# Eight unused columns between two buffers of the second model

## The chip, the cores and the metric

The kernel runs on one core of one Trainium2 chip. The metric is the device time of one launch in microseconds (us), the median of several runs. Engines are named as the profile names them: PE is the matrix engine (PEld its weight loads), DVE the vector engine, ACT the scalar engine, POOL the GpSimd engine, SP the queue that issues most transfers.

## The reference

Two models run one after the other, all in float32, on 256 tokens of width 1024, two layers each.

The first block projects x with `w_in` and runs four branches (a recurrent one, a latent attention, a convolution, a cross-attention into a memory), gates and adds them, projects with `w_out` and normalises. The second block takes its result, and a context of 256 more tokens beside it. Cut to what matters here:

```python
def swiglu(h, w1, w2):
    gate, up = jnp.split(h @ w1, 2, axis=-1)
    return (jax.nn.silu(gate) * up) @ w2

def ffn_sublayer(h, m, sub, g_pre, g_post, w1, w2):
    shift, scale, gate = mods_of(m, sub)
    y = swiglu(modulate(rms_norm(h, g_pre[sub]), shift, scale), w1, w2)
    return h + MACARON_WEIGHT * gate * rms_norm(y, g_post[sub])

def hybrid_layer(x, xc, ...):
    x, xc = ffn_sublayer(x, ..., 0, ...), ffn_sublayer(xc, ..., 0, ...)
    ...                      # projections h @ w_in, three kinds of attention, o @ w_out
    x = ffn_sublayer(x, ..., 2, ...)
    ...                      # the same for xc, in the first layer alone
```

The inner width of the feed-forward part is 22 x 128 = 2816.

## The kernel before, in words

**Products in parts.** The type `fp32r` is a rounded float32 that PE takes at a faster rate. To keep the precision, every large product of the second model is made of three: a weight panel is split into a high part and a low part (the rest), the activations likewise, and high x high, high x low and low x high are added in one bank of PSUM. In `parts` these are lines L1830, L1831 and L1832: the weights are the stationary operand, which is loaded anew for every matmul, and the activations the moving one, of 512 columns (the tokens of x and of the context) or of 256.

```python
1828            def parts(out, w, w_low, a, a_low, start, stop):
...
1830                mm(out, w, a, start=start, stop=False)
1831                mm(out, w, a_low, start=False, stop=False)
1832                return mm(out, w_low, a, start=False, stop=stop)
```

`mm(out, stationary, moving)`. In the second half of a feed-forward part, and in the output projection of an attention, the roles are changed: `rows_tile` (matmul on L1913) has the activations (`hs`, or `aT` and `aT_low`) stationary and 512 columns of the split weights `ws` moving. The first model does the same with its own buffers on L477 (`xT` moving), L478 (`xT_low` moving) and L479 (`xT` moving), with `ws` stationary and 256 columns each. Its other matmuls, such as L444 and L454, are plain float32.

**Flow of a panel.** A panel is 128 x 2048 float32 (1 MB). SP brings it into one of two slots of `ring`; POOL waits for it and for the matmuls that used the slot of `ws` last (`come`, L1758 is a one-element operation after the wait), writes the high part (L1745) and then the low part (L1747) and raises `split_in`; PE waits for `split_in` and does 48 matmuls. From the second panel of the last feed-forward part on (`SHARED`), POOL makes only half of the low part (L1763, L1765), and DVE the other half (L2445). PE counts `used` up at a panel's last matmul, and this lets POOL split the panel after the next.

**Order of the stages in the second model.** For each layer: feed-forward with 22 panels of `unit_panel` (the first two in `lead`, which starts on 256 tokens while the other 256 are still being normalised) and 11 panels of `rows_tile`; the attention, with 8 panels of projections (again behind a `lead`), 2 of values, plain float32 matmuls on `hidT`, `prob` and `y`, and 4 panels of `rows_tile`; and a feed-forward part again. The last one has 256 tokens instead of 512.

**Where the buffers lie.** Buffers are laid out one behind the other in every partition, in the order of their declarations. The second model's are:

```python
1635        ring = sb("ring", [P, 2, PAN])
1636        ws = sb("ws", [P, 2, 2, PAN], F32R)
1637        y = sb("y", [P, 4, D])
1638        aT = sb("aT", [P, KD, T2], F32R)
1639        hidT = sb("hidT", [P, FF, T2])
```

and then `sg`, `rows`, `bias`, `aT_low`, `prob` (in one place with `hs`), `gsc`, `gg`, `gg_rows` and `small`. Byte addresses in a partition, in the built programs, and the rest on division by 64:

| buffer | role in split products | address | mod 64 |
|---|---|---|---|
| second model `ws` | weights' parts | 54048 | 32 |
| `y` | (not in split products) | 86816 | 32 |
| `aT` | activations, high | 103200 | 32 |
| `aT_low` | activations, low | 189216 | 32 |
| `hs` | hidden activations, both parts | 205600 | 32 |
| first model `ws` | weights' parts | 153216 | 0 |
| first model `xT` | activations, high | 107296 | 32 |
| first model `xT_low` | activations, low | 202368 | 0 |

Inside a buffer, every operand of these matmuls starts a whole multiple of 512 bytes behind the buffer's start, so all operands of a buffer share its rest. The plain float32 matmul of L454 has `brT` (116640) and `ring` (25376), both with rest 32.

Of the kernel before, what the change touches and what calls it, by code (L numbers as in the profile page):

```python
# [15 lines left out]
P = 128  # L16
# [1610 lines left out]
def second_model(nc, io, x_tok, mod, early, out):  # L1627

    with ExitStack() as ctx:
        def sb(name, shape, dt=F32):  # L1630
            return ctx.enter_context(nc.sbuf_tensor("m2_" + name, shape, dt))
# [3 lines left out]
        ring = sb("ring", [P, 2, PAN])  # L1635
        ws = sb("ws", [P, 2, 2, PAN], F32R)
        y = sb("y", [P, 4, D])
        aT = sb("aT", [P, KD, T2], F32R)
        hidT = sb("hidT", [P, FF, T2])
        sg = sb("sg", [P, 2, T2])  # L1640
# [982 lines left out]
def program(nc, io, out):  # L2623

    with ExitStack() as ctx:
        x_tok = ctx.enter_context(nc.sbuf_tensor("x_tok", [P, NT, D], F32))
        mod = ctx.enter_context(nc.sbuf_tensor("mod", [P, DEPTH * 9 * KD * 2], F32))
        early = {"vec": ctx.enter_context(nc.sbuf_tensor("m2_vec", [P, NVEC2], F32)),
                 "con": ctx.enter_context(nc.sbuf_tensor("m1_con", [P, NCON], F32)),
                 "mem": ctx.enter_context(nc.sbuf_tensor("memT_ctx", [P, NT * D], F32)),  # L2630
                 "loaded": ctx.enter_context(nc.semaphore("m2_loaded"))}
        first_model(nc, io, x_tok, mod, early)
        second_model(nc, io, x_tok, mod, early, out)
# [16 lines left out]
```

How the kernel before makes its waits and increments, by code:

```python
        @block.sync  # L336
# [12 lines left out]
            sp.dma_start(early["vec"][:, :], io["vec2"]).then_inc(early["loaded"], 16)  # L349
            def panels(g0, g1):
                with sp.Fori(g0, g1) as g:
                    for p in range(RING):
                        sp.wait_ge(s["panel_used"], (g - 1) * RING + p + 1)
                        sp.dma_start(ring[:, p, :], io["panels1"][bass.ds(g * RING + p, 1), :, :]
                                     .rearrange("o p n -> p (o n)")).then_inc(slot[p], 16)
            panels(1, PANELS1 // RING)
            for n in range(PANELS1, PANELS1 + RING):
                sp.wait_ge(s["panel_used"], n - RING + 1)
                if n == PANELS1:
                    sp.dma_start(ring[:, 0, 0:PAN // 2], io["panels1"][n, :, 0:PAN // 2]).then_inc(s["first_in"], 16)
                    sp.dma_start(ring[:, 0, PAN // 2:], io["panels1"][n, :, PAN // 2:]).then_inc(slot[0], 16)
                else:
                    sp.dma_start(ring[:, n % RING, :], io["panels1"][n, :, :]).then_inc(slot[n % RING], 16)
            panels(PANELS1 // RING + 1, DEPTH * PANELS1 // RING)
            sp.dma_start(early["mem"][:, :].rearrange("p (i d) -> p i d", d=D), io["ctx"]).then_inc(early["loaded"], 16)
            if out is not None:
                sp.wait_ge(s["layer_done"], DEPTH + 1)
                sp.dma_start(out[0, :, :].rearrange("(i p) d -> p i d", p=P), x_tok[:, :, :]).then_inc(s["out_st"], 16)
                sp.wait_ge(s["out_st"], 16)
```

## Time and profile before

| | |
|---|---|
| time, median of 3 runs | 2860.42 us (2859.85 to 2860.79) |
| span of the profiled execution | 2857.6 us |
| PE busy, share of the span | 96% |
| PE weight loads busy | 80% |
| POOL / DVE / ACT busy | 47% / 36% / 23% |
| DMA | 390.24 MB, mean 137 GB/s |

The profiled execution has its span alone, not a device time of its own beside it; the median of the three runs is 2.8 us longer than the span. The recorded duration of a matmul includes its way through the array, so matmuls overlap and their rate is read from their starts, not from their durations.

### The profile page before, as it was taken

To read this page: it belongs to the slowest core of one execution; us is meant where nothing else is said; L and a number is where in the kernel's file an instruction comes from. 1 tells how busy PE (TensorE), PEld (TensorE's weight loads), DVE (VectorE), ACT (ScalarE), POOL (GpSimd) and SP (SyncE) were. 2 spreads that over 40 slices of the span, in tenths; PEclk is the share of its full clock that TensorE was granted. 3 is DMA by queue.
4 is the path that set the end of the run, shared out by engine and by line. 5 is a ranking of instruction groups with operands and counts; after the bars stand their busy time and mean duration, and the time that the engine had idled before them with its cause. 6 is when DMAs were issued, how large, how long until landed. Compare 5 with 4: busy or idle time off the path is not lost.

```text
span 2857.6 us, 44212 instructions
## 1 busy us (share of the span) xinstructions
PE 2737.9 (96%) x17521; PEld 2281.5 (80%) x17521; DVE 1019.0 (36%) x1586; ACT 656.3 (23%) x1220; POOL 1342.8 (47%) x608
## 2 busy tenths in 40 slices
PE   8999999999999897999999999999999999898998
PEld 7987778699777775888888778888888888776996
DVE  1752753247438333001340533002330023524237
ACT  4432212144322112000131443001130001415101
POOL 4830100067010003565646555666646666667786
PEclk9999999999999998999999999999999999999999
DMA  6556633445565444323222123222223222232453
GB/s 231 187 193 249 258 141 134 183 177 187 224 238 209 160 163 120 110 94 103 88 89 103 45 67 104 90 101 94 98 89 103 90 101 97 96 117 71 151 171 138
DMA packets 68621, 390.24 MB, mean 137 GB/s; under 512 B 19232, under 2 KB 20864, under 8 KB 22528
## 3 DMA queue, kind: packets, MB, share of 16 engines
q1 hardware_dynamic: 66640, 379.03, 37.1%
q10 hardware_dynamic: 1840, 9.18, 0.9%
q8 instruction: 106, 1.74, 0.2%
q14 instruction: 35, 0.29, 0.0%
HBM read 387.09 MB, written 1.10 MB: 136 GB/s over the span
## 4 chain that ended last, share of the span: by engine, by line
issue 26%; POOL 11%; POOLq 10%; PE 9%; DMA 3%; DVE 1%; SPq 1%; ACT 0%; DVEq 0%; ACTq 0%
POOL m_ws L1747 9%; POOLq L1746 7%; DMA m_ring<-in_panels 3%; PE m_bank L1913 2%; POOLq L1759 1%; PE m_bank L1830 1%; POOL m_ws L1765 1%; PE m_bank L1831 1%; PE m_bank L1832 1%; POOLq L1764 1%; PE m_bank L2046 1%; SPq L1703 1%; PE m_bank L2058 1%; PE m_bank L2009 1%; PE m_bank L2010 1%
## 5 line engine op out<-in xcount | busy, mean ns | idle before, releaser
L1830 PE MATMUL m_bank<-m_aT,m_ws 128*128 128x512 f32 (+1 forms) x1792 | 631.4, 352 | 34.8 <-DVE m_aT_low L2408 15.6
L1831 PE MATMUL m_bank<-m_aT_low,m_ws 128*128 128x512 f32 (+1 forms) x1792 | 628.0, 350 | 0.0
L1832 PE MATMUL m_bank<-m_aT,m_ws 128*128 128x512 f32 (+1 forms) x1792 | 627.7, 350 | 0.0
L1747 POOL TENSOR_TENSOR m_ws<-m_ring,m_ws 128x2048 fp32r<-128x2048 f32 x127 | 593.5, 4673 | 18.7
L1913 PE MATMUL m_bank<-m_ws,m_hs 128*128 128x512 f32 x1848 | 422.6, 390 | 3.5 <-DVE m_ws L2445 1.5
L1830 PEld LDWEIGHTS m_bank<-m_aT,m_ws 128*128 128x128 f32 x1792 | 344.9, 192 | 82.2 <-issue 23.6
L1913 PEld LDWEIGHTS m_bank<-m_ws,m_hs 128*128 128x128 f32 x1848 | 346.1, 188 | 79.4 <-issue 6.9
L383 POOL TENSOR_TENSOR m_ws<-m_ring,m_ws 128x2048 fp32r<-128x2048 f32 x48 | 221.3, 4627 | 342.4 <-ACT m_ws L910 342.4
L1831 PEld LDWEIGHTS m_bank<-m_aT_low,m_ws 128*128 128x128 f32 x1792 | 345.1, 193 | 42.4
L1832 PEld LDWEIGHTS m_bank<-m_aT,m_ws 128*128 128x128 f32 x1792 | 344.9, 192 | 42.6
L2451 DVE TENSOR_TENSOR m_hidT<-m_sg,m_bank 128x512 f32 (+3 forms) x88 | 54.7, 621 | 687.6 <-ACT m_sg L2218 687.6
L1758 POOL TENSOR_TENSOR m_small<-m_small 128x1 f32<-128x1 f32 x158 | 31.9, 202 | 546.5 <-PE m_bank L1832 366.4
L1745 POOL TENSOR_SCALAR m_ws<-m_ring 128x2048 fp32r<-128x2048 f32 x127 | 243.4, 1916 | 24.9 <-issue 20.0
L444 PE MATMUL m_bank<-m_xF,m_ring 128*128 128x256 f32 x1024 | 229.1, 382 | 4.2 <-DMA m_ring<-in_panels 4.2
L444 PEld LDWEIGHTS m_bank<-m_xF,m_ring 128*128 128x128 f32 x1024 | 191.9, 190 | 46.6 <-issue 12.1
L2218 ACT ACTIVATE m_sg<-m_bank 128x512 f32<-128x512 f32 (+1 forms) x88 | 48.0, 545 | 764.4 <-PE m_bank L1832 764.4
L2458 DVE TENSOR_TENSOR m_hs<-m_hidT,m_hs 128x512 fp32r<-128x512 f32 (+1 forms) x88 | 144.9, 1657 | 206.5 <-ACT m_hs L2222 206.1
L477 PE MATMUL m_bank<-m_xT,m_ws 128*128 128x256 f32 x752 | 212.2, 282 | 1.4 <-ACT m_work L928 1.4
L479 PE MATMUL m_bank<-m_xT,m_ws 128*128 128x256 f32 x752 | 212.8, 283 | 0.0
L478 PE MATMUL m_bank<-m_xT_low,m_ws 128*128 128x256 f32 x752 | 209.0, 278 | 0.0
L477 PEld LDWEIGHTS m_bank<-m_xT,m_ws 128*128 128x128 f32 x752 | 141.4, 188 | 3.2 <-ACT m_work L928 3.0
L478 PEld LDWEIGHTS m_bank<-m_xT_low,m_ws 128*128 128x128 f32 x752 | 141.3, 188 | 0.2
(350 smaller groups left out, 3412.9 us busy)
## 6 DMA issues: line engine op xcount, KB each, us to landing
m_ring<-in_panels SPq DMA_DIRECT2D x350, 1024.0 KB, 4.9
m_rows<-m_gg_dram ACTq DMA_DIRECT2D x6, 1024.0 KB, 5.4
m_bias<-in_rpb SPq DMA_DIRECT2D x48, 64.0 KB, 2.7
m_ring<-in_panels SPq DMA_DIRECT2D x4, 512.0 KB, 5.4
m_hT<-in_ln_rows ACTq DMA_DIRECT2D x2, 1024.0 KB, 6.8
m_con<-in_con SPq DMA_DIRECT2D x1, 1536.0 KB, 10.7
memT_ctx<-in_memT SPq DMA_DIRECT2D x2, 512.0 KB, 5.6
x_tok<-in_x SPq DMA_DIRECT2D x1, 1024.0 KB, 13.6
```

Source lines behind the costliest of these rows:

```text
L383: nc.gpsimd.tensor_tensor(ws[:, c_ % 3, 1, :], ring[:, PANEL[("in", c_)] % RING, :], ws[:, c_ % 3, 0, :].bitcast(F32), ALU.subtract).then_ ...
L444: last = mm(out[:, u * T:(u + 1) * T], w[:, u, k, :], xF[:, k, :], start=(k == 0), stop=(k == KD - 1))
L477: mm(dst, w[:, 0, u, k, :], xT[:, k, :], start=(k == 0), stop=False)
L478: mm(dst, w[:, 0, u, k, :], xT_low[:, k, :], start=False, stop=False)
L479: last = mm(dst, w[:, 1, u, k, :], xT[:, k, :], start=False, stop=(k == KD - 1))
L1745: nc.gpsimd.tensor_scalar(ws[:, p, 0, :], ring[:, p, :], 1.0, 0.0, ALU.mult, ALU.add)
L1746: pool.drain()
L1747: nc.gpsimd.tensor_tensor(ws[:, p, 1, :], ring[:, p, :], ws[:, p, 0, :].bitcast(F32), ALU.subtract)\
L1830: mm(out, w, a, start=start, stop=False)
L1831: mm(out, w, a_low, start=False, stop=False)
L1832: return mm(out, w_low, a, start=False, stop=stop)
L1913: last = mm(bank[:, 2 * i + hf, :], lhs[:, at], rhs[:, hf * 512:(hf + 1) * 512], start=start and q == 0, stop=stop and q == 2)
```

## The change

One declaration is added, of eight float32 columns (32 bytes in a partition) that nothing reads or writes:

```diff
@@ -1635,6 +1635,7 @@
         ring = sb("ring", [P, 2, PAN])
         ws = sb("ws", [P, 2, 2, PAN], F32R)
         y = sb("y", [P, 4, D])
+        sb("between", [P, 8])
         aT = sb("aT", [P, KD, T2], F32R)
         hidT = sb("hidT", [P, FF, T2])
         sg = sb("sg", [P, 2, T2])
```

`aT`, `hidT`, `sg`, `rows`, `bias`, `aT_low`, `prob`, `hs` and all behind them move by 32 bytes: `aT` to 103232, `aT_low` to 189248 and `hs` to 205632, each with rest 0 on division by 64. `ring`, `ws` and `y` of the second model, and all buffers of the first, stay. No instruction is added, removed or moved on any engine; lines behind L1637 have a number that is higher by one.

## Rows read from the trace of the kernel before

**Rows 1.** Page: span, and busy time of the engines.

```profile
span 2857.6 us, 44212 instructions
PE 2737.9 (96%) x17521; PEld 2281.5 (80%) x17521; DVE 1019.0 (36%) x1586; ACT 656.3 (23%) x1220; POOL 1342.8 (47%) x608
```

**Rows 2.** Groups on PE by shape: line, out<-in, shape xcount | busy us, mean ns | idle before.

```profile
L1830 PE MATMUL m_bank<-m_aT,m_ws 128*128 128x512 f32 x1088 | 423.8, 390 | 6.7 <-POOL m_ws L1747 3.8 <-DVE m_hidT L2451 2.9
...
L1913 PE MATMUL m_bank<-m_ws,m_hs 128*128 128x512 f32 x1848 | 422.6, 390 | 3.5 <-DVE m_ws L2445 1.5 <-issue 1.3 <-POOL m_ws L1765 0.5
...
L1830 PE MATMUL m_bank<-m_aT,m_ws 128*128 128x256 f32 x704 | 207.6, 295 | 28.2 <-DVE m_aT_low L2408 15.6 <-POOL m_ws L1747 6.0 <-POOL m_ws L1765 4.6
...
L1913 PE MATMUL m_bank<-m_ws,m_aT 128*128 128x512 f32 x192 | 53.0, 398 | 1.8 <-POOL m_ws L1747 1.8
```

**Rows 3.** Timeline of PE, 1200:1240: start us, duration; 174 matmuls lie between these starts.

```profile
1199.90 0.39 PE L1830 MATMUL m_bank<-m_aT,m_ws 128*128 128x512 f32 x1
...
1239.34 0.39 PE L1830 MATMUL m_bank<-m_aT,m_ws 128*128 128x512 f32 x1
```

**Rows 4.** Timeline of PE, 1499:1511, 256 columns; 87 matmuls from start to start.

```profile
1498.87 0.28 PE L1830 MATMUL m_bank<-m_aT,m_ws 128*128 128x256 f32 x1
...
1509.31 0.28 PE L1830 MATMUL m_bank<-m_aT,m_ws 128*128 128x256 f32 x1
```

**Rows 5.** Timeline of PE, 1362:1400, 169 matmuls merged into one row.

```profile
1361.74 38.47 PE L1913 MATMUL m_bank<-m_ws,m_hs 128*128 128x512 f32 x169
```

**Rows 6.** Timeline of PE, 507:520, plain float32, 62 matmuls in one row.

```profile
506.80 13.54 PE L454 MATMUL m_bank<-m_brT,m_ring 128*128 128x256 f32 x62
```

**Rows 7.** Timeline of PE, 60:75, first model; 126 matmuls from start to start.

```profile
60.06 0.28 PE L477 MATMUL m_bank<-m_xT,m_ws 128*128 128x256 f32 x1
...
74.90 0.28 PE L477 MATMUL m_bank<-m_xT,m_ws 128*128 128x256 f32 x1
```

**Rows 8.** Timeline of PE, 105:107, first model, four matmuls in a row.

```profile
105.09 0.28 PE L478 MATMUL m_bank<-m_xT_low,m_ws 128*128 128x256 f32 x1
105.20 0.28 PE L479 MATMUL m_bank<-m_xT,m_ws 128*128 128x256 f32 x1
105.32 0.28 PE L477 MATMUL m_bank<-m_xT,m_ws 128*128 128x256 f32 x1
105.44 0.28 PE L478 MATMUL m_bank<-m_xT_low,m_ws 128*128 128x256 f32 x1
```

**Rows 9.** Timeline of PE, 1724:1725, with the clock granted at half speed.

```profile
1723.98 0.41 PE L1830 MATMUL m_bank<-m_aT,m_ws 128*128 128x256 f32 x1
1724.20 0.41 PE L1831 MATMUL m_bank<-m_aT_low,m_ws 128*128 128x256 f32 x1
```

**Rows 10.** Timeline of POOL, 1800:1825, a feed-forward part with 512 tokens; [idle before <- what ended it].

```profile
1805.49 0.19 POOL L1758 TENSOR_TENSOR m_small<-m_small 128x1 f32<-128x1 f32 x1 [3.86 <-PE m_bank L1832]
1805.84 1.92 POOL L1745 TENSOR_SCALAR m_ws<-m_ring 128x2048 fp32r<-128x2048 f32 x1 [0.16 <-issue]
1807.91 4.60 POOL L1747 TENSOR_TENSOR m_ws<-m_ring,m_ws 128x2048 fp32r<-128x2048 f32 x1
```

**Rows 11.** Timeline of all engines, 1748.9:1751.2, end of a lead.

```profile
1748.99 0.28 PE L1832 MATMUL m_bank<-m_aT,m_ws 128*128 128x256 f32 x1
...
1750.72 0.49 PE L1830 MATMUL m_bank<-m_aT,m_ws 128*128 128x512 f32 x1 [1.45 <-DVE m_hidT L2451]
```

**Rows 12.** Timeline of PE, last feed-forward part: starts of three panels.

```profile
2697.39 0.38 PE L1830 MATMUL m_bank<-m_aT,m_ws 128*128 128x256 f32 x1 [0.32 <-POOL m_ws L1765]
...
2703.24 0.28 PE L1830 MATMUL m_bank<-m_aT,m_ws 128*128 128x256 f32 x1
...
2709.48 0.38 PE L1830 MATMUL m_bank<-m_aT,m_ws 128*128 128x256 f32 x1 [0.32 <-POOL m_ws L1765]
```

**Rows 13.** Timeline of POOL in the same stretch.

```profile
2703.49 0.19 POOL L1758 TENSOR_TENSOR m_small<-m_small 128x1 f32<-128x1 f32 x1 [0.55 <-PE m_bank L1832]
...
2709.25 0.19 POOL L1758 TENSOR_TENSOR m_small<-m_small 128x1 f32<-128x1 f32 x1
```

## The prediction

> **What bounds the kernel now.** I read the page first: PE is busy for 96% of the span, no other engine for more than half [rows 1]. So what counts is how long PE takes for one matmul, and where something else sets the pace. The groups by shape show where PE's time lies in the second model: 1088 matmuls of 512 columns on each of L1830, L1831 and L1832 with `aT` or `aT_low` moving, 704 of 256 columns on each, and 1848 + 192 on L1913 with `ws` moving [rows 2]. Idle time stands before few of them: 6.7 us before the 512-column ones.
>
> Then the timeline of PE, for the rate. With 512 columns, 174 matmuls take 1239.34 - 1199.90 = 39.44 us, 226.7 ns each [rows 3]; with 256 columns, 87 take 10.44 us, 120.0 each [rows 4]. L1913 runs at (38.47 - 0.39) / 168 = 226.7 as well [rows 5]. At 2.4 GHz 512 columns last 213.3 ns and 256 columns 106.7. Both forms therefore pay 13.3 ns over their columns, 32 columns' worth. Plain float32 shows that this isn't the price of loading weights: 62 matmuls with as many weight loads take 13.54 us; with about 0.4 taken off for the last one's own length (0.39 in [rows 3]), 61 steps of 215 ns each [rows 6], only 2 over the 213.3 of two passes over 256 columns. Nor is it paid at the lower clock: 0.22 us from start to start where 256 columns at 1.2 GHz last 213.3 ns [rows 9]. What is paid looks like the fetching of fp32r operands, which at the full clock takes as long as the array, or longer.
>
> **What 32 bytes are worth.** The buffers of the second model all have rest 32 on division by 64; the change makes the activations' 0. The trace of before has one place with other rests: the first model, with `ws` at 0, `xT` at 32 and `xT_low` at 0. There 126 matmuls of the same 256 columns take 14.84 us, 353.3 ns for each three [rows 7], not 360.0. So a rest does matter: a group of three with one moving operand at 0 is 6.7 ns shorter, just 16 columns, which are 64 bytes. My reading is that the moving operand is fetched in pieces of 64 bytes: one that starts at rest 32 touches one piece more (17 instead of 16, or 33 instead of 32), and each piece lasts 16 columns, 6.67 ns. Every matmul then pays one piece, and one with the moving operand at rest 32 two. All three counts come out: 3 x (106.7 + 13.3) = 360, 2 x 120.0 + 113.3 = 353.3, and 213.3 + 13.3 = 226.7. Where the starts can be told apart it is L478, the one with `xT_low`, that is short: 0.11 us to the next start, the others 0.12 [rows 8]. The first model's float32 matmuls, with both operands at 32, pay nothing because each column there lasts two passes, which hides the piece.
>
> The Trainium skill weighs against this. Its page "TensorE: Matmul & The Clock Gate", section "Wait — 56ns, not 53.3ns?", gives N / 2.4 + about 2.5 ns for a warm matmul, wherever its operands lie; [rows 3] has 226.7 where that would give 215.8, so it doesn't describe these fp32r matmuls. Its page "SBUF — State Buffer", section "Specifications (TRN2)", has lines of 16 bytes; a shift of 32 bytes would then change nothing. That would make the time of before, and is counted as a rival.
>
> **The sum.** L1913 keeps its moving operand `ws` at 32, and gets nothing; the same holds for all of the first model and all plain float32. For L1830 to L1832:
>
> 1. 512 columns: 3 x 1088 = 3264 matmuls x 6.67 = **21.8 us**. All of it should be seen: a panel is 48 x 226.7 = 10.88 us, POOL splits one in 0.19 + 0.16 + 1.92 + 0.15 + 4.60 = 7.0 and then waits 3.86 us for PE [rows 10]. A panel of 10.56 us leaves it 3.5. ACT and DVE wait for PE there too, since 6.7 us in all is PE's idle time before these [rows 2].
> 2. Five leads with 4 x 48 = 192 matmuls of 256 columns, at most 960 x 6.67 = 6.4 us. But the last 48 of a lead are followed by a wait, 1748.99 to 1750.72 [rows 11], because POOL could begin only at the end of the 48 before them; it needs its 7.0 us against 48 x 120 = 5.76, so what those 48 gain the wait takes. The first ones run at the lower clock [rows 9] or wait for DVE (15.6 us in all [rows 2]). I count half of the rest, 72: 72 x 6.67 = 0.48 us, five times: **2.4 us**, with bounds of 0 and 6.4.
> 3. 96 matmuls of 256 columns in the second attention: two panels of 5.76 us, under POOL's 7.0, so **0**.
> 4. The last feed-forward part, 22 panels of 48 matmuls with 256 columns. Here PE and POOL alternate: two panels last 2709.48 - 2697.39 = 12.09 us [rows 12]. POOL starts at 2703.49, when PE's panel ends, and has done at 2709.25, 5.76 us later; PE goes on after it at 2709.48 [rows 12, 13]. The ring is one panel of PE (5.76), one of POOL (5.76), and 0.57 for handing over. A panel that is 0.32 shorter makes it 11.77; two panels of POOL, 11.52, still fit. So half of the 0.64 is got: 10.5 pairs x 0.32 = **3.4 us**, with bounds of 0 and 7.0.
>
> Together 21.8 + 2.4 + 3.4 = 27.6 us off the profiled execution's span of 2857.6, which gives 2830.0, and with the 2.8 us around it **2832.8**. By the bounds this case alone lies between 2860.4 - 35.2 = 2825.2 and 2860.4 - 21.8 = 2838.6.
>
> What else moves is DVE's, ACT's and POOL's operands in `hidT`, `sg`, `prob` and `hs`, and the targets of the `bias` and `rows` transfers. No row compares two rests for these. I count nothing: beside the 512-column matmuls they lie under PE's work, which idles 6.7 us there. Where that cover is gone PE idles before L1830 for 28.2 us in the whole kernel, 15.6 of them for DVE [rows 2]; a tenth more or less of it would be 3 us either way.
>
> **The rivals.**
>
> *It is the distance between stationary and moving operand that matters* (they meet in the same place of the memory when the rests are equal). Then the first model's three are 2 q + 120.0 = 353.3, so q = 116.7, 3.3 less. After the change both kinds of matmul have unequal rests: 3264 x 3.33 = 10.9, L1913 2040 x 3.33 = 6.8, leads 1.2, the last part 1.7; 20.6 in all, **2839.8**. Against it: L478, with equal rests, would be the long one of the three, and it is the short one [rows 8]. The skill's TensorE page, section "Step-by-step: what each phase is for", has separate ports for the two operands, which would also exclude it; no run here shows ports. Chance 0.17.
>
> *Nothing changes.* The first model's 353.3 may come from something other than rests (its three slots of `ws`, its PSUM halves), or the piece is 128 bytes or more long, and rest 64 is as bad as rest 32; against the last speaks that 128 bytes would cost 32 columns. Here also: only the stationary operand's rest counts, 120.0 - 117.8 = 2.2 ns each, and only L1913's moves, 2040 x 2.2 = 4.5 us, 2855.9. **2860**, 2856 to 2861, chance 0.22.
>
> *Slower: a matmul pays more when its two operands have different rests.* Suppose that L478 in the first model, with both at 0, costs the bare 106.7 + 2; then L477 and L479 cost (353.3 - 108.7) / 2 = 122.3, 2.3 more than 120.0. After the change all split matmuls of the second model are of that kind: 3264 x 2.3 + 2040 x 2.3 = 12.2, leads 1, last part 1 (POOL's ring as above): 14 us, **2874.5**. It makes the kernel slower by over 0.2% from 0.9 ns a matmul on. For it: 0.12 against 0.11 [rows 8] fits it as well. Chance 0.08.
>
> *The forecast*: 0.50. The rest of 0.03 is for gains that meet an unseen wait.
>
> **How the numbers follow.** The forecast and the first rival are both faster: 0.67, with 0.02 of the rest 0.69. No change (2856 to 2861) holds 0.22, and slower, with 0.01 of the rest, 0.09. 0.2% is 5.7 us, about what a measurement of this kernel tells from no change. The range has to take in the forecast's bounds (from 2825), the first rival and no change to leave out less than 2 in 10: 2824 to 2861. The likeliest case's own range is 2825 to 2839.
>
> **What the profile would show.** Step by step: L1831 (now L1832) to the next start 220.0 ns with 512 columns, 660 for three, where 680 stood; 113.3 with 256; L1913 (now L1914) still 226.7. If L1914 falls to about 223 and the others to 223 too, it was the distance. POOL's wait [rows 10] shrinks from 3.86 to 3.5 us; the wait behind a lead grows from 1.7 to 2.0; the pair of panels [rows 12] becomes 11.8. The forecast is wrong if the 512-column matmuls stay at 226.7, or if they fall while POOL or DVE gets slower by as much.

## The result and the profile after

The changed kernel takes 2891.04 us (median of 4 runs, 2888.13 to 2891.84), the kernel before 2860.14 in the same comparison: a ratio of 1.0108, with a 95% interval of 1.0094 to 1.0123. It is slower by 31 us; 2832.8 was forecast, and a range up to 2861.

The page has the same instructions, 32.4 us more span and 28 us more of PE; DVE, ACT and POOL are as busy as before to 2.3 us [rows 1]:

```profile
span 2890.0 us, 44212 instructions
PE 2766.1 (96%) x17521; PEld 2273.6 (79%) x17521; DVE 1016.9 (35%) x1586; ACT 656.8 (23%) x1220; POOL 1345.1 (47%) x608
```

In the groups on PE by shape (all lines behind L1637 are one higher) both kinds of 512-column matmul have grown, `aT` moving from 390 to 395 ns and `hs` stationary from 390 to 396, while the idle time before them has grown by 0.8 us in all [rows 2]:

```profile
L1914 PE MATMUL m_bank<-m_ws,m_hs 128*128 128x512 f32 x1848 | 433.9, 396 | 3.8 <-DVE m_ws L2446 1.8 <-issue 1.5 <-POOL m_ws L1766 0.5
L1831 PE MATMUL m_bank<-m_aT,m_ws 128*128 128x512 f32 x1088 | 430.3, 395 | 7.2 <-POOL m_ws L1748 7.2
```

The timeline of PE gives the rate. First `aT` moving, 512 columns: 171 matmuls from start to start take 39.90 us, 233.3 ns each, where it was 226.7 [rows 3]. Then 256 columns, 63 matmuls in 7.42 us, 117.8 each, where it was 120.0 [rows 4]. Then one merged row of L1914: (42.40 - 0.39) / 180 = 233.4, where it was 226.7 [rows 5]:

```profile
1200.06 0.40 PE L1831 MATMUL m_bank<-m_aT,m_ws 128*128 128x512 f32 x1
...
1239.96 0.39 PE L1831 MATMUL m_bank<-m_aT,m_ws 128*128 128x512 f32 x1
...
1512.00 0.28 PE L1831 MATMUL m_bank<-m_aT,m_ws 128*128 128x256 f32 x1
...
1519.42 0.28 PE L1831 MATMUL m_bank<-m_aT,m_ws 128*128 128x256 f32 x1
...
1367.82 42.40 PE L1914 MATMUL m_bank<-m_ws,m_hs 128*128 128x512 f32 x181
```

So a matmul of 512 columns lost 6.7 ns and one of 256 gained 2.2. The loss stands in 3264 + 2136 matmuls (1848 with `hs`, 192 with `aT` and 96 with `aT_low` stationary) and in 192 more, L2009 to L2011 of before, which have `aT` and `aT_low` stationary too; those went from 227.2 to 233.2 ns. Of the 5592, the 264 of the last feed-forward part took 65.3 us before and 66.1 now, 0.8 more. The others make 5328 x 6.67 = 35.5 us, 36.3 together. The gain is small: two panels of the last feed-forward part start 12.02 us apart instead of 12.09 [rows 12], in all 0.7 us, and the five leads can give back 960 x 2.2 = 2.1 at most. These sums leave 33.5 us for a span that grew by 32.4. POOL's wait per panel went from 3.86 us up to 4.16, while its own longest operation stayed at 4.60 to 4.63 [rows 10]: the growth is PE's.

```profile
2729.63 0.38 PE L1831 MATMUL m_bank<-m_aT,m_ws 128*128 128x256 f32 x1 [0.46 <-POOL m_ws L1766]
...
2741.65 0.38 PE L1831 MATMUL m_bank<-m_aT,m_ws 128*128 128x256 f32 x1 [0.45 <-POOL m_ws L1766]
```

The first model's buffers have not moved. Yet in this execution 126 of its matmuls take 14.98 us, 356.7 ns for three, where the kernel before had 353.3 in the same stretch [rows 7]:

```profile
59.97 0.28 PE L477 MATMUL m_bank<-m_xT,m_ws 128*128 128x256 f32 x1
...
74.95 0.28 PE L477 MATMUL m_bank<-m_xT,m_ws 128*128 128x256 f32 x1
```

That is half of the 6.7 ns from which the forecast was drawn, with nothing changed there. From 94 us on, in the same execution, the same lines take 353.3 again.

### The profile page after: what moved, and what is told of

The parts are those of the page before. It is cut to its first block, busy times and chain, and to the rows that moved or that the text cites. A ratio compares the mean times of both kernels' runs of the same rounds, so it can differ in the third digit from the quotient of the medians.

```text
span 2890.0 us, 44212 instructions
## 1 busy us (share of the span) xinstructions
PE 2766.1 (96%) x17521; PEld 2273.6 (79%) x17521; DVE 1016.9 (35%) x1586; ACT 656.8 (23%) x1220; POOL 1345.1 (47%) x608
## 4 chain that ended last, share of the span: by engine, by line
issue 27%; POOL 11%; POOLq 10%; PE 9%; DMA 3%; DVE 1%; SPq 1%; ACT 0%; DVEq 0%; ACTq 0%
POOL m_ws L1748 9%; POOLq L1747 7%; DMA m_ring<-in_panels 3%; PE m_bank L1914 2%; POOLq L1760 1%; PE m_bank L1831 1%; PE m_bank L1833 1%; PE m_bank L1832 1%; POOL m_ws L1766 1%; POOLq L1765 1%; PE m_bank L2047 1%; SPq L1704 1%; PE m_bank L2059 1%; PE m_bank L2010 1%; PE m_bank L2012 1%
## 5 line engine op out<-in xcount | busy, mean ns | idle before, releaser
L1831 PE MATMUL m_bank<-m_aT,m_ws 128*128 128x512 f32 (+1 forms) x1792 | 635.4, 355 | 36.6 <-DVE m_aT_low L2409 15.6
L1914 PE MATMUL m_bank<-m_ws,m_hs 128*128 128x512 f32 x1848 | 433.9, 396 | 3.8 <-DVE m_ws L2446 1.8
L1914 PEld LDWEIGHTS m_bank<-m_ws,m_hs 128*128 128x128 f32 x1848 | 346.4, 188 | 90.6 <-issue 6.6
L1831 PEld LDWEIGHTS m_bank<-m_aT,m_ws 128*128 128x128 f32 x1792 | 341.9, 191 | 92.2 <-issue 24.8
L444 PE MATMUL m_bank<-m_xF,m_ring 128*128 128x256 f32 x1024 | 229.1, 382 | 4.2 <-DMA m_ring<-in_panels 4.2
L477 PE MATMUL m_bank<-m_xT,m_ws 128*128 128x256 f32 x752 | 212.8, 283 | 1.4 <-ACT m_work L928 1.4
L479 PE MATMUL m_bank<-m_xT,m_ws 128*128 128x256 f32 x752 | 212.4, 282 | 0.0
L478 PE MATMUL m_bank<-m_xT_low,m_ws 128*128 128x256 f32 x752 | 209.4, 278 | 0.0
L477 PEld LDWEIGHTS m_bank<-m_xT,m_ws 128*128 128x128 f32 x752 | 141.2, 188 | 3.2 <-ACT m_work L928 3.0
L478 PEld LDWEIGHTS m_bank<-m_xT_low,m_ws 128*128 128x128 f32 x752 | 141.6, 188 | 0.2
```

The source lines that it names most:

```text
L444: last = mm(out[:, u * T:(u + 1) * T], w[:, u, k, :], xF[:, k, :], start=(k == 0), stop=(k == KD - 1))
L477: mm(dst, w[:, 0, u, k, :], xT[:, k, :], start=(k == 0), stop=False)
L478: mm(dst, w[:, 0, u, k, :], xT_low[:, k, :], start=False, stop=False)
L479: last = mm(dst, w[:, 1, u, k, :], xT[:, k, :], start=False, stop=(k == KD - 1))
L1914: last = mm(bank[:, 2 * i + hf, :], lhs[:, at], rhs[:, hf * 512:(hf + 1) * 512], start=start and q == 0, stop=stop and q == 2)
```

## The experiments

Two theories at first. **D**: what counts is the distance of the stationary from the moving operand. **R**: the place of one of the two counts by itself. "Distance" below is the start of the moving operand less that of the stationary one, in bytes; before, all of the second model's split products had a distance of 0 modulo 512. Where a time from start to start is given for a block, it is a mean over the block, from the trace's nanoseconds; one worked out from a row shown here can differ from it by half a nanosecond.

**The same shift for everything (e_all), and for the weights' parts alone (e_ws).**

```diff
+        sb("between", [P, 8])          # e_all: in front of ring, none in front of aT
         ring = sb("ring", [P, 2, PAN])
...
+        sb("between", [P, 8])          # e_ws: in front of ws ...
         ws = sb("ws", [P, 2, 2, PAN], F32R)
         y = sb("y", [P, 4, D])
+        sb("behind", [P, 8])           # ... and behind y
```

> The eight unused columns stand in front of ring instead, so that ring, ws, y and all activations of the second model move by 32 bytes together and have rest 0. Theory D: the time of before, 2860, and 226.7 ns for each 512-column split matmul. Theory R (a rest of 0 for the activations is what costs): like the changed kernel, 2891. My first reading (a moving operand at rest 0 saves a piece): below 2835, since ws as the moving operand of L1913 has rest 0 too.

> Eight unused columns in front of ws and eight behind y: ws moves by 32 bytes to rest 0, the activations by 64 and keep their rest 32. Theory D: like the changed kernel, about 2891, with 233.3 ns for 512 columns. Theory R on the activations' rest: the time of before, 2860. If the price depends on which operand has which rest, another time than either.

Measured: e_all 2858.93 us, ratio 0.9999 (0.999 to 1.0009); e_ws 2891.21, ratio 1.0111 (1.0095 to 1.0128). Timeline of PE for e_all, 177 matmuls, 226.7 ns each:

```profile
1199.70 0.39 PE L1831 MATMUL m_bank<-m_aT,m_ws 128*128 128x512 f32 x1
...
1239.82 0.39 PE L1831 MATMUL m_bank<-m_aT,m_ws 128*128 128x512 f32 x1
```

and for e_ws, 171 matmuls, 233.3:

```profile
1199.92 0.39 PE L1832 MATMUL m_bank<-m_aT,m_ws 128*128 128x512 f32 x1
...
1239.82 0.40 PE L1832 MATMUL m_bank<-m_aT,m_ws 128*128 128x512 f32 x1
```

In e_all the activations stand where the changed kernel has them, and nothing is lost; in e_ws their rest is that of before, and all is lost. Theory R falls, for either operand, and with it my piece of 64 bytes.

**Blocks of matmuls with every other engine idle (probe_off, probe_n).** Two buffers and a block per line, between the two models:

```diff
+            for k in range(24): mm(out[:, k % 8, 0:512], w(0, k), a(32, k, 512), start=True, stop=True)
...
         first_model(nc, io, x_tok, mod, early)
+        offsets(nc, x_tok)
```

`w(at, k)` is 128 columns of an fp32r buffer that start `at` bytes behind its (k % 4) x 512 bytes, `a(at, k, n)` n columns behind (k % 4) x 2048. Both buffers start at a multiple of 1024 bytes.

> The kernel of before with 28 blocks of 24 fp32r matmuls of 512 columns each put between the two models, while every other engine is idle; stationary and moving operand start at chosen bytes behind two buffers that both lie at a multiple of 1024. Theory D (what counts is whether the two operands have the same rest on division by 64): 226.7 ns from start to start wherever the difference of the two offsets is a multiple of 64, about 233.3 where it is 32, and something between or like it at 4, 8, 16; the pair (32, 32) is as good as (0, 0). Theory R (what counts is the rest of one operand alone): the pairs (0, 0) and (32, 32) differ by 6.7 ns, and (0, 32) equals either one of them. Theory C (the loss needs other engines' traffic): 216 to 227 everywhere.

> The kernel of before with blocks of 24 fp32r matmuls between the two models, of 64 to 512 columns, with the moving operand 0 or 32 bytes off the stationary one's rest. Theory D with a fixed price at equal rests and a price in proportion at unequal ones, as 120.0 and 226.7 against 116.7 and 233.3 suggest: N / 2.4 + 13.3 ns at equal rests, N / 2.4 x 35/32 at unequal ones, which cross at 341 columns (155.5 ns): at 320 unequal rests are still faster (145.8 against 146.7), at 384 slower (175.0 against 173.3). Theory R or a piece per matmul: the difference between the two rests is the same for all N.

Timeline of PE, one merged row for a block; (duration - 0.39) / 23 is the time from start to start. The pairs (stationary, moving) are, from the top: (0, 0), (0, 32), (0, 64), (0, 128), (0, 256), (32, 32), (32, 96), (16, 16), (16, 32):

```profile
1103.97 5.60 PE L2650 MATMUL pr_out<-pr_a,pr_w 128*128 128x512 f32 x24
...
1137.38 5.76 PE L2656 MATMUL pr_out<-pr_a,pr_w 128*128 128x512 f32 x24
...
1154.31 5.66 PE L2659 MATMUL pr_out<-pr_a,pr_w 128*128 128x512 f32 x24
...
1165.41 5.76 PE L2661 MATMUL pr_out<-pr_a,pr_w 128*128 128x512 f32 x24
1171.01 5.62 PE L2662 MATMUL pr_out<-pr_a,pr_w 128*128 128x512 f32 x24
...
1204.14 5.63 PE L2668 MATMUL pr_out<-pr_a,pr_w 128*128 128x512 f32 x24
...
1220.76 5.66 PE L2671 MATMUL pr_out<-pr_a,pr_w 128*128 128x512 f32 x24
...
1237.46 5.71 PE L2674 MATMUL pr_out<-pr_a,pr_w 128*128 128x512 f32 x24
1243.01 5.60 PE L2675 MATMUL pr_out<-pr_a,pr_w 128*128 128x512 f32 x24
```

PE alone shows it all: 5.60 is 226.5 ns, 5.76 is 233.5, 5.66 is 229.1. No traffic of other engines is needed. The period isn't the 64 bytes that I had expected: from a stationary start of 0, a distance of 64 costs 2.6 ns and 128 the full 7, and only 256 (227.3), 512 and 1024 (226.7) are as good as 0. In 26 blocks of 512 columns at other places none was faster than (0, 0).

The last two rows don't fit theory D: (16, 16) has distance 0 and took 231.0 ns, (16, 32) has distance 16 and took 226.7, where (0, 16) had 231.8 and (32, 48) 231.4. So the distance alone tells the price only for starts at multiples of 32 bytes, which all operands of the split products in the kernels have. What the start itself does at odd multiples of 16 stays open.

probe_n: 120.9 ns against 116.8 with 256 columns at distances 0 and 32, 146.4 against 146.9 with 320, 174.5 against 173.3 with 384, 206.2 against 204.4 with 448, 227.5 against 233.4 with 512. A price in proportion to the columns, with a crossing at 341, is wrong: up to 448 columns a distance of 32 is as good or better, and it loses at 512. (With fewer than 256 columns the clock went to its lower level in most blocks, with a mean of 0.57 from 1110 to 1130 us, so these tell nothing.)

**256 and 128 bytes in the real kernel (e_256b, e_128b).**

```diff
-        sb("between", [P, 8])
+        sb("between", [P, 64])         # e_128b: 32
```

> 64 unused columns, 256 bytes, instead of eight. If the price follows the distance of the operands modulo 256, as the blocks of probe_off have it (226.7 at 256, 512 and 1024, but 233.3 at 128 and 229.1 at 64): the time of before, 2860. If any distance other than the old one costs: about 2891.

> 32 unused columns, 128 bytes. All buffers keep their rest on division by 64 and by 128. Modulo 64 or 128 (my theory D in its first form): the time of before, 2860. Modulo 256: about as slow as the changed kernel, 2885 to 2892, since a block of probe_off at 128 had 233.3.

Measured: 2860.61 us, ratio 1.0006 (0.9996 to 1.0015), and 2889.05, ratio 1.0105 (1.0088 to 1.0122). Timeline of PE for e_256b, 174 matmuls, 226.7 each:

```profile
1199.89 0.39 PE L1831 MATMUL m_bank<-m_aT,m_ws 128*128 128x512 f32 x1
...
1239.33 0.39 PE L1831 MATMUL m_bank<-m_aT,m_ws 128*128 128x512 f32 x1
```

and for e_128b, 171 matmuls, 233.4 each:

```profile
1199.62 0.40 PE L1831 MATMUL m_bank<-m_aT,m_ws 128*128 128x512 f32 x1
...
1239.53 0.39 PE L1831 MATMUL m_bank<-m_aT,m_ws 128*128 128x512 f32 x1
```

The period is 256 bytes, and theory D as I had it (modulo 64) is mended by that.

**One half of the move at a time (e_hs, e_unit).**

```diff
+        sb("between", [P, 8])          # e_unit alone: in front of aT
         aT = sb("aT", [P, KD, T2], F32R)
...
+        sb("between", [P, 8])          # e_hs: 8; e_unit: "behind", 56, so that hs moves by 256 bytes
         with ExitStack() as attention:
```

> The eight unused columns stand in front of prob and hs, so only hs (and the small buffers behind it) moves: ws and aT keep equal rests, ws and hs don't. Theory D: L1831 to L1833 (the split matmuls with aT) at 226.7, L1914 with hs stationary 6.5 ns slower, 1848 x 6.5 = 12 us: 2872. A theory in which the place of the moving operand counts (ws, not moved): the time of before.

> The other part alone: eight columns in front of aT, and 56 more in front of prob and hs, so that hs lies 256 bytes further and keeps its distance modulo 256. Theory D: the 512-column matmuls with aT moving at 233.3, hs stationary at 226.7 as before; the rest of the 31 us, 19: 2879. The two parts should add up to the change. If something else of the move costs (DVE, ACT or transfers at other places), they don't.

Measured: e_hs 2870.66 us, ratio 1.004 (1.0025 to 1.0054); e_unit 2878.78, ratio 1.0067 (1.005 to 1.0083). With 2859.12 before, that is 11.5 and 19.7 us, 31.2 together; the change took 30.9. Timelines of PE, L1914 in e_hs, (38.66 - 0.39) / 164 = 233.4 ns:

```profile
1361.63 38.66 PE L1914 MATMUL m_bank<-m_ws,m_hs 128*128 128x512 f32 x165
```

and the same line in e_unit, (38.47 - 0.39) / 168 = 226.7:

```profile
1371.70 38.47 PE L1915 MATMUL m_bank<-m_ws,m_hs 128*128 128x512 f32 x169
```

In e_hs `ws` is the moving operand and stays where it was; its stationary partner alone moves, and the matmul pays in full. That is the step that I had put at nothing.

**Is there a direction? (e_64b)**

```diff
-        sb("between", [P, 8])
+        sb("between", [P, 16])
```

> 16 unused columns, 64 bytes. The blocks of the probes say that here the direction counts: stationary at 32 and moving at 96 had 228.8, stationary at 96 and moving at 32 had 233.3. So the matmuls with aT moving should come near 229 (3264 x 2.1 = 7 us) and L1914 (hs stationary, ws moving) near 233 (13 us): 2880. Modulo 64 instead: 2860. Unequal places alone, without direction: 2891.

Measured: 2880.09 us, ratio 1.0072 (1.0057 to 1.0087). Timeline of PE, `aT` moving (174 matmuls, 228.9 ns each) and L1914 ((38.43 - 0.39) / 163 = 233.4):

```profile
1199.62 0.39 PE L1831 MATMUL m_bank<-m_aT,m_ws 128*128 128x512 f32 x1
...
1239.44 0.39 PE L1831 MATMUL m_bank<-m_aT,m_ws 128*128 128x512 f32 x1
...
1371.81 38.43 PE L1914 MATMUL m_bank<-m_ws,m_hs 128*128 128x512 f32 x164
```

The blocks' numbers hold in the kernel: a distance of +64 costs 2.2 ns, one of -64 the full 6.7.

**What collides? (probe_width, probe_turns)** More blocks, with lines such as

```diff
+            for k in range(24): mm(out[0:32, k % 8, 0:512], w(0, k)[:, 0:32], a(32, k, 512), start=True, stop=True)
...
+            for k in range(32): mm(out[:, k % 8, 0:512], w(32 * (k % 2), k), a(32 * (k % 2), k, 512), start=True, stop=True)
```

> Blocks of 24 matmuls between the models again, every other engine idle. First more distances at 512 columns (160, 192, 224, 12, 20, 40 bytes, and the stationary operand moved instead, by 64 and 128, or both): modulo 256, 192 should be like 64 (229) and 160 and 224 like 32 or 96 (233.3); both moved by 64 or 128 gives 226.7. Then stationary operands of 32, 64, 96 and 128 columns, each at distance 0 and 32. If the loss comes from loading the next weights while the moving operand is read, a narrower load costs less, and the difference of 6.7 ns shrinks with the width; if it comes from the moving operand alone, width changes nothing. Then plain float32 of 256 and 512 columns at distance 0 and 32: 215.7 and 429 at both, if two passes give the reads enough room. Last the same two operands over and over: as with changing ones.

> Blocks of 32 matmuls between the models, every other engine idle. In the first ones both operands change their place by 32 bytes from one matmul to the next. In step (0, 0), (32, 32): a matmul's own operands are at distance 0, but its moving operand is at distance 32 from the next matmul's weights. Out of step (0, 32), (32, 0): the other way round. Theory L (the moving operand is read while the next matmul's weights are loaded, and these two collide): in step 233.3, out of step 226.7 with 512 columns. Theory O (a matmul's own pair counts): in step 226.7, out of step 233.3. If only one operand changes its place, every other pair is at distance 32 in either theory: half the price, 230. The same with 256 columns (120.0 and 116.7) and with 128 bytes. Then 256 columns at distances 0 to 224 in steps of 32, and 416, 480, 496, 504 and 508 columns at distances 0 and 32: does a distance of 32 lose only at 512 columns, where the moving operand is a multiple of 256 bytes long, or from about 500 on?

Timeline of PE for probe_width: stationary operands of 32 columns at distances 0 and 32, of 128 columns at 0 and 32, then plain float32 of 256 columns at 0 and 32:

```profile
1184.95 5.71 PE L2664 MATMUL pr_out<-pr_a,pr_w 128*32 128x512 f32 x24
1190.51 5.74 PE L2665 MATMUL pr_out<-pr_a,pr_w 128*32 128x512 f32 x24
...
1218.28 5.62 PE L2670 MATMUL pr_out<-pr_a,pr_w 128*128 128x512 f32 x24
1223.73 5.77 PE L2671 MATMUL pr_out<-pr_a,pr_w 128*128 128x512 f32 x24
1229.34 10.52 PE L2672 MATMUL pr_out<-pr_a,pr_w 128*128 128x256 f32 x48
1239.69 10.52 PE L2673 MATMUL pr_out<-pr_a,pr_w 128*128 128x256 f32 x48
```

The narrow operand shrinks the difference between the distances, from 6.2 ns with 128 columns to 3.0 with 96 and 1.0 with 64 and with 32, as expected if the weights' loading is a party to it, but in the wrong manner: it is distance 0 that gets dearer (231.4 with 32 columns, against 227.2 with 128), while distance 32 stays near where it was (232.4 against 233.4). The expectation that less loading costs less fell. Plain float32 takes 215.8 ns at either distance, as forecast; the profile shows each such product as two records, 48 for the 24 of a block. Distances 160, 192 and 224 had 234.1, 233.3 and 233.1; my 229 for 192 was wrong, since 192 is -64, the dear direction: (96, 32) had 233.2 here, and e_64b, which ran later, shows it in the kernel. Both operands moved by 64 or by 128 had 227.3 and 228.9, and 226.7 and 226.8 over the second half of the block: as good as (0, 0), as expected.

Timeline of PE for probe_turns, in step and out of step:

```profile
1110.14 7.58 PE L2650 MATMUL pr_out<-pr_a,pr_w 128*128 128x512 f32 x32
1117.56 7.57 PE L2651 MATMUL pr_out<-pr_a,pr_w 128*128 128x512 f32 x32
```

(7.58 - 0.39) / 31 = 231.9 and 231.6 ns: neither L nor O. With the stationary operand alone changing its place it was 234.1, with the moving one alone 231.0, where both theories had 230. A matmul's own pair and its neighbour's weights both seem to count, or neither is the right description. At distance 32, 480, 496, 504 and 508 columns had 217.8, 224.3, 226.9 and 230.2 ns against 216.7, 223.6, 226.7 and 228.4 at 0: a loss of about 1 ns or less up to 504 columns, 1.8 at 508 and 6 to 7 at 512.

**Placing the 256-column matmuls (e_best, probe_192, e_192, e_192b).** In the last feed-forward part the tokens take other columns of `aT` and `aT_low`; in the first model unused columns move `xT_low` (e_best, e_192) and `ws` (e_192):

```diff
+        def tokens_at(e, st):
+            lo = st * T + (8 if SUBS[e][2] == NT else 0)      # e_192, e_192b: 48
+            return slice(lo, lo + T)
...
+            place.enter_context(nc.sbuf_tensor("m1_before", [P, 8], F32))   # e_192: 48; not in e_192b
             work = place.enter_context(nc.sbuf_tensor("m1_work", [P, 73 * T], F32))
         ws = sb("ws", [P, 3, 2, PAN], F32R)
+        sb("between", [P, 8])                                 # e_192: 48; not in e_192b
```

e_192 also has 56 unused columns in front of both, so that `ws` starts at 96 modulo 256 and `xT` and `xT_low` at 32.

> Both kernels' good places together: 512-column split matmuls keep distance 0 (226.7), 256-column ones get distance 32 where that is possible. In the last feed-forward part the 256 tokens stand in columns 8 to 263 of aT and aT_low; in the first model eight unused columns between ws and xT_low (and eight in front of work, so that its parts stay clear of xT_low) put xT_low at distance 32 instead of 0. Theory D modulo 256: L478's stretch 350.0 instead of 353.3 for three, 752 x 3.3 = 2.5 us; the last part 116.7 instead of 120.0, of which POOL's ring gives back half, 10.5 x 0.16 = 1.7 us. Together 4 us, 2856: at the edge of what can be timed, but plain in the profile. If distances don't matter one by one, nothing.

e_best: 2858.10 us, ratio 0.9998 (0.9989 to 1.0006): the 4 us of the sum did not come, or can't be told from none. The first model's three took 355.0 ns, not 350, though both rates that it had before (353.3 and 356.7) were gone; so `xT` at distance 160 doesn't cost what 32 costs, and my q of 116.7 for it was never measured; a block at (0, 160), run later in probe_192, had 117.4.

> Blocks of 32 matmuls of 256 columns at distances 0 to 240 in steps of 16, then at distance 192 from other starts (32, 64, 96, 128, 160, and 448 for 192 + 256), with the operands exchanged (stationary at 192, 64 or 32, moving at 0), and 320 columns at distance 192. If the distance decides: 113.3 at 192 from every start and at 448, and something else for the exchanged ones but for stationary 64, moving 0, which is 192 modulo 256. If one place decides: 113.3 at (0, 192) alone.

Timeline of PE, blocks of 32, (duration - 0.28) / 31: (0, 0), (0, 64), (0, 192), (64, 256), (96, 32):

```profile
1107.62 4.00 PE L2650 MATMUL pr_out<-pr_a,pr_w 128*128 128x256 f32 x32
...
1122.77 3.79 PE L2654 MATMUL pr_out<-pr_a,pr_w 128*128 128x256 f32 x32
...
1152.88 3.80 PE L2662 MATMUL pr_out<-pr_a,pr_w 128*128 128x256 f32 x32
...
1171.53 3.93 PE L2667 MATMUL pr_out<-pr_a,pr_w 128*128 128x256 f32 x32
...
1201.37 3.79 PE L2675 MATMUL pr_out<-pr_a,pr_w 128*128 128x256 f32 x32
```

Distance 192 takes 113.3 to 114.1 ns for five pairs (114.2 for 448) and 117.8 for three others, (64, 256), (128, 320) and (64, 0). Distance 64 took 113.4 at (0, 64) here, 117.8 at (192, 0), and 117.8 at (0, 64) in probe_n and probe_turns. So at 256 columns a distance of 64 or 192 allows two rates, and which one a stretch gets, the place doesn't settle alone.

> The 256-column split matmuls at distance 192, the 512-column ones at 0. First model: unused columns so that ws starts at 96 modulo 256 and xT and xT_low at 32; last feed-forward part: its 256 tokens in columns 48 to 303 of aT and aT_low. If the blocks' 113.3 holds in the kernel: 340 instead of 353.3 for three in the first model, 752 x 13.3 = 10 us, and in the last part half of 48 x 6.7 ns a panel, 3.4 us: 2847. If engines at work take it away, or POOL, which splits a panel of the first model in 4.6 us against PE's 5.4, becomes the bound: 2852 to 2860.

> The last feed-forward part alone at distance 192: two panels in 11.77 us instead of 12.09 (48 x 113.3 = 5.44 for PE, 5.76 for POOL, 0.57 to hand over), 3.4 us less, 2856.5. In the first model 353.3, as before.

e_192: 2849.92 us (median of 6, 2842.69 to 2851.84), ratio 0.9965 (0.9953 to 0.9977): faster than both kernels. e_192b: 2857.70, ratio 0.9994 (0.9985 to 1.0003), which can't be told from none. Timeline of PE for e_192, first model (L480 is L477 of before), 123 matmuls in 13.94 us, 340.0 ns for three:

```profile
59.84 0.28 PE L480 MATMUL m_bank<-m_xT,m_ws 128*128 128x256 f32 x1
...
73.78 0.28 PE L480 MATMUL m_bank<-m_xT,m_ws 128*128 128x256 f32 x1
```

That is the 10 us, as expected: 752 x 13.3 ns in the execution that was profiled, which took 2842.69 us, the shortest of the six. The last part differs between the two kernels, although its distance is 192 in both. In e_192b two panels last 12.01 us, and the 94 steps between the second and the third row here take 117.8 ns each:

```profile
2693.90 0.38 PE L1834 MATMUL m_bank<-m_aT,m_ws 128*128 128x256 f32 x1 [0.44 <-POOL m_ws L1769]
2694.12 0.28 PE L1835 MATMUL m_bank<-m_aT_low,m_ws 128*128 128x256 f32 x1
...
2705.19 0.28 PE L1836 MATMUL m_bank<-m_aT,m_ws 128*128 128x256 f32 x1
...
2705.91 0.38 PE L1834 MATMUL m_bank<-m_aT,m_ws 128*128 128x256 f32 x1 [0.44 <-POOL m_ws L1769]
```

In e_192 two panels last 11.87 us (2694.30 to 2706.17), and 46 steps within a panel take 113.7 each:

```profile
2694.52 0.28 PE L1838 MATMUL m_bank<-m_aT_low,m_ws 128*128 128x256 f32 x1
...
2699.75 0.28 PE L1839 MATMUL m_bank<-m_aT,m_ws 128*128 128x256 f32 x1
```

So the two rates of probe_192 both turn up here. With 117.8 the forecast's ring gives 5.65 + 5.76 + 0.57 = 11.98, with 113.7 it gives 11.79, 0.08 under what e_192 took. e_192b missed its 11.77 because PE ran at the slower of the two rates, and not because the ring was wrong. Why one kernel gets the one and the other the other is not shown.

## Why the prediction was wrong

- **What bounds the kernel**: right. PE's own rate was the thing to look at, with 226.7 and 120.0 ns; the change stands in that rate. PE's idle time before L1831 went from 34.9 to 36.6 us, so waits had a small part in it.
- **"My reading is that the moving operand is fetched in pieces of 64 bytes"** is the step that failed. It rested on one sample of other places, the first model's 353.3 ns against 360.0. Three arithmetic fits (120, 113.3, 226.7) looked like evidence, but they were one number fitted with one free size. The same buffers ran at 356.7 in the changed kernel's trace, and `xT` stood at distance 160, not 32, modulo the 256 bytes that turned out to count. e_all (226.7 ns, with both operands moved) and e_ws (233.3, with the activations' rest kept) refute the reading in the second model: what counts there is where one operand stands against the other.
- **"L478 is the short one of the three"** [rows 8], the evidence that set the forecast above the distance rival, holds for one stretch alone. From 95 to 135 us the steps behind L477, L478 and L479 are 119.3, 112.3 and 121.7 ns. From 60 to 93 us of the same trace, where the 353.3 of [rows 7] was taken, they are 118.3, 117.7 and 117.3, and none is short:

```profile
70.07 0.28 PE L478 MATMUL m_bank<-m_xT_low,m_ws 128*128 128x256 f32 x1
70.19 0.28 PE L479 MATMUL m_bank<-m_xT,m_ws 128*128 128x256 f32 x1
70.31 0.28 PE L477 MATMUL m_bank<-m_xT,m_ws 128*128 128x256 f32 x1
```

- **Term 1, 21.8 us for 512 columns**: the size was right and the sign wrong. The rule was carried from 256 columns, where another distance does gain (120.0 to 117.8 in the kernel), to 512, where it loses 6.7 ns a matmul. No row of before showed 512 columns at another distance, and this should have stood as an unknown with both signs.
- **L1913 "gets nothing"**: wrong. e_hs shows 11.5 us for a move of its stationary operand alone. The count of such matmuls, here and in the rivals, also left out 96 on L1913 with `aT_low` and 192 on L2009 to L2011.
- **Terms 2 to 4**: the ring of PE and POOL in the last part did keep most of a faster PE for itself (12.09 to 12.02 us for 2.2 ns a matmul, half of which would be 11.98). What the leads gave back was not measured by itself. DVE, ACT, POOL and transfers at other places cost nothing that shows: e_all puts `hidT`, `sg`, `prob` and `hs` at the very places of the changed kernel and takes the time of before (0.999 to 1.0009), and the two halves of the move add up.
- **The distance rival** had the right variable and carried the same error, 116.7 at 256 taken for a gain at 512. **The slower rival** ("a matmul pays more when its two operands have different rests") was what happened at 512 columns, in both roles, at 6.7 ns instead of 2.3, though with rests modulo 256 and not 64 (e_128b); it had a chance of 0.08. **Plain float32** untouched: right.

What stays open is what collides. That PE alone shows the whole effect, that it shows with fp32r and not with plain float32, and that it depends on both operands is shown. It is also gone at the lower clock: 256-column matmuls of the leads take 213.3 ns there in both kernels, at distance 0 and at 32. That the reading of one matmul's moving operand meets the loading of weights is only argued, and probe_turns and probe_width fit neither simple form of it. Nor is it known what picks one of two steady rates at the same addresses.

## What to carry to other kernels

Where fp32r matmuls run back to back, take their time from start to start and compare it among buffers before any of them is moved: the distance between the two operands, modulo 256 bytes here and for starts at multiples of 32, is worth 3% of a 512-column matmul and up to 6% of a 256-column one, so an unused or a resized buffer anywhere in front of one of them changes the time. Keep 512-column pairs at distance 0; for 256 columns try distances in short blocks and then in the kernel, as e_192 did for 8.6 us and e_192b for nothing that shows. Look at more than one stretch of the trace, since the same matmuls can run at two rates in one execution. Don't carry a rate from one size or one place to another on a single sample, however well the arithmetic comes out.

## What the runs showed of the hardware

- fp32r matmuls with new weights each, 512 columns, starts at multiples of 32 bytes, distance modulo 256: 226.7 ns at 0, about 229 at +64 (228.9 in the kernel), 233.3 at 32, -64 and 128. Off those starts, 239.7 at (0, 20), 231.0 at (16, 16) and 226.7 at (16, 32). With 256 columns: 120.0 at 0, 116.5 to 118 at 32, 113.3 or 117.8 at 64 and 192.
- The same addresses can run at two steady rates: 353.3 and 356.7 ns for three matmuls in the first model, both within one execution of the changed kernel; 113.4 and 117.8 in a block.
- Plain float32 takes 215.8 ns a record for 256 columns, two records a product, at distance 0 and at 32.
- At the lower clock, 256-column fp32r matmuls take 213.3 ns at distance 0 and at 32.
- A stationary operand of 32 columns instead of 128 made a 512-column matmul slower at distance 0, 231.4 instead of 227.2.
